# Two query projections of the sparse attention moved between the indexer's dot products

## The reference, cut to what matters

```python
h = rms_norm(x, norm_mix[l])
z = h @ w_in[l]
(g_q, g_k, g_v, g_lr, g_r, d_q, d_k, d_v, i_q, i_k, i_w, c_u) = jnp.split(z, split_at, axis=-1)
dq = rms_norm(d_q.reshape(B, S, DSA_HEADS, DSA_DH), dsa_qnorm[l])    # 6 heads of 64
dk = rms_norm(d_k.reshape(B, S, DSA_HEADS, DSA_DH), dsa_knorm[l])
# per block of 128 queries; qx: 8 indexer heads of 64
dots = jnp.einsum('bthd,bsd->bths', qx, k_idx_f) * (IDX_DIM ** -0.5)
score = jnp.einsum('bths,bth->bts', jax.nn.relu(dots), wx)
score = jnp.where(key_pos[None, :] <= tpos[:, None], score, -jnp.inf)
_, sel = lax.top_k(score, topk)                                      # topk = 128
```

## Time and profile before

| | |
|---|---|
| median of 3 runs | 1573.6 us (1568.34 to 1575.02) |
| span of the profiled execution | 1572.3 us |
| its own whole time | not given beside the span; the span is 1.3 us under the median |
| PE busy | 1479.6 us, 94% |
| DVE busy | 1202.7 us, 76% |
| ACT busy | 884.6 us, 56% |
| POOL busy | 550.9 us, 35% |
| mean granted TensorE clock | 0.971 of full speed |

### The profile page before, as it was taken

The page is one execution under the profiler, slowest core; times in us unless marked ns, Lnnn a source line. Parts: engine busy times, 40 slices in busy tenths (PEclk is TensorE's granted clock), DMA queues, the critical chain, the costliest instruction groups (busy, mean ns, idle before and its releaser), DMA issues.

```text
span 1572.3 us, 20276 instructions
## 1 busy us (share of the span) xinstructions
PE 1479.6 (94%) x6710; PEld 1072.5 (68%) x6710; DVE 1202.7 (76%) x1762; ACT 884.6 (56%) x1286; POOL 550.9 (35%) x250
## 2 busy tenths in 40 slices
PE   7999999999899999999889999989998989999996
PEld 4687565557577888777556865556575778787773
DVE  4697499634469999999758965895335799999997
ACT  5642233563548787888475513235534478878881
POOL 2243113250004665553542421231600046654444
PEclk9999989999889999999999999899999899999998
DMA  6243301230427999999651530013113289999995
GB/s 221 88 107 133 121 1 54 88 103 1 161 100 287 393 398 400 398 399 399 206 181 42 124 129 0 1 54 134 57 35 127 107 322 399 399 399 399 399 399 193
DMA packets 151484, 312.73 MB, mean 199 GB/s; under 512 B 33158, under 2 KB 46380, under 8 KB 151228
## 3 DMA queue, kind: packets, MB, share of 16 engines
q1 hardware_dynamic: 140300, 271.39, 47.6%
q0 software_dynamic: 6624, 24.12, 4.1%
q10 hardware_dynamic: 4496, 16.40, 2.6%
HBM read 287.76 MB, written 29.50 MB: 202 GB/s over the span
## 4 chain that ended last, share of the span: by engine, by line
PE 47%; DVE 26%; DMA 16%; issue 6%; ACT 4%; DVEq 1%; POOL 0%; SPq 0%; POOLq 0%; ACTq 0%
PE ps L654 11%; DMA arena<-in_w_down 11%; DVE rest_w_down L1334 7%; PE ps L671 6%; PE ps L1411 4%; DMA arena<-in_w_gate 3%; DVE rest_w_up L1334 3%; DVE rest_w_gate L1334 3%; PE ps L1433 3%; DVE mixr L1144 2%; PE ps L733 2%; DVE xg_rest L1347 2%; PE ps L674 2%; PE ps L760 2%; ACT head_w_down L1329 2%
## 5 line engine op out<-in xcount | busy, mean ns | idle before, releaser
L1997 POOL TENSOR_TENSOR rest_w_down<-arena,head_w_down 128x2048 fp32r<-128x2048 f32 x30 | 187.6, 6252 | 196.1 <-ACT head_w_down L1329 196.1
L1334 DVE TENSOR_TENSOR rest_w_down<-arena,head_w_down 128x2048 fp32r<-128x2048 f32 x30 | 150.7, 5023 | 14.7 <-ACT head_w_down L1329 14.5
L1334 DVE TENSOR_TENSOR rest_w_gate<-arena,head_w_gate 128x2048 fp32r<-128x2048 f32 x64 | 145.9, 2280 | 0.1
L1334 DVE TENSOR_TENSOR rest_w_up<-arena,head_w_up 128x2048 fp32r<-128x2048 f32 x64 | 143.5, 2282 | 0.1
L1329 ACT ACTIVATE head_w_gate<-arena 128x2048 fp32r<-128x2048 f32 x60 | 115.0, 1920 | 40.7 <-DMA arena<-in_w_gate 40.6
L1329 ACT ACTIVATE head_w_down<-arena 128x2048 fp32r<-128x2048 f32 x60 | 115.2, 1927 | 38.4 <-DMA arena<-in_w_down 37.7
L1329 ACT ACTIVATE head_w_up<-arena 128x2048 fp32r<-128x2048 f32 x64 | 122.1, 1943 | 9.3 <-DMA arena<-in_w_up 9.2
L671 PE MATMUL ps<-hT,arena 128*128 128x512 f32 x224 | 108.6, 616 | 0.0
L1318 PE MATMUL ps<-head_w_gate,xg_head 128*128 128x512 f32 x256 | 104.0, 406 | 4.2 <-DVE xg_rest L1347 3.0
L1308 PE MATMUL ps<-head_w_down,he_head 128*128 128x512 f32 x240 | 99.6, 415 | 6.8 <-DVE rest_w_down L1334 3.7
L1144 DVE SCALAR_TENSOR_TENSOR mixr<-arena,cf,mixr 128x512 f32<-128x512 f32 x120 | 98.4, 820 | 4.3
(11 more groups left out here) (365 smaller groups left out, 3595.9 us busy)
## 6 DMA issues: line engine op xcount, KB each, us to landing
arena<-in_w_gate SPq DMA_DIRECT2D x64, 1024.0 KB, 10.3
arena<-in_w_up SPq DMA_DIRECT2D x64, 1024.0 KB, 11.0
arena<-in_w_down SPq DMA_DIRECT2D x64, 1024.0 KB, 10.5
arena<-in_w_in SPq DMA_DIRECT2D x10, 1536.0 KB, 6.8
yrows<-yb ACTq DMA_DIRECT2D x30, 512.0 KB, 6.3
arena<-in_w_in SPq DMA_DIRECT2D x4, 2048.0 KB, 8.0
x<-in_x SPq DMA_DIRECT2D x8, 512.0 KB, 13.5
arena<-in_w_in SPq DMA_DIRECT2D x16, 256.0 KB, 4.9
```

Of the source, the lines that this page charges most:

```text
L1334: nc.vector.tensor_tensor(wl[q][:, c, :], raw[q][:, c, :], wh[q][:, c, :].bitcast(F32), ALU.subtract).then_inc(s_split[q], 1)
L1997: nc.gpsimd.tensor_tensor(wl[2][:, c, :], raw[2][:, c, :], wh[2][:, c, :].bitcast(F32), ALU.subtract)\
```

## The change

PE's program alone is changed. Job 5 and job 6 are no longer projected behind the dots; behind every second dot stands one chunk of them, three matmuls: 16 chunks behind 16 pairs of dots. `project` and `split_project` take a range of chunks for that. The programs of ACT, DVE, POOL and SP are as before.

```diff
-                def split_project(n):
+                def split_project(n, chunks=range(KD)):
...
-                    for c in range(KD):
+                    for c in chunks:
...
-                    last.then_inc(sN["proj_done"], 1)
+                    if KD - 1 in chunks:
+                        last.then_inc(sN["proj_done"], 1)
...
-                        split_project(n)
+                        split_project(n, chunks)
...
                     nc.tensor.matmul(ps[4 + n % 4][:, 0:P * (i + 1)], iq[r, h // 2, P * i:P * i + P],
                                      ik2[r, 0:P * (i + 1)], start=True, stop=True).then_inc(sN["dots_done"], 1)
+                    if n % 2:
+                        c = n // 2
+                        project(AFTER_IDX + c // KD, range(c % KD, c % KD + 1))
...
-                project(AFTER_IDX)
                 pe.wait_ge(sN["relu_done"], len(DOTS))
                 for n in range(6):
-                    project(AFTER_IDX + 1 + n)
+                    if n:
+                        project(AFTER_IDX + 1 + n)
                     head_sum(n)
```

## The result

The changed kernel takes 1594.6 us (median of 4 runs, 1593.62 to 1601.21), the kernel before beside it 1572.8 (4 runs, 1568.34 to 1575.02). The ratio is 1.0159, 95% interval 1.0133 to 1.0184: slower by 21.7 us, where 11.8 were forecast, and 0.6 us outside the range.

A forecast was written before the change was run, and what follows sets the result against it. PE, busy for 94% of the span, was taken to bound the kernel. ACT's uncovered chain (4.2 us) and the clock (1.7) gave 5.9 us per layer, 11.8 in all, so 1585 us, range 1575 to 1594.

The forecast's parts named there:

- Term 1: PE's dots and projections together: 25.8 us against 26.0 now, row changes of 0.29 us replacing the waits; nothing gained.
- Term 2: ACT's weights head, copy and square no longer hidden behind jobs 5 and 6: first sum of squares 4.2 us late.
- Term 3: PE's clock at half speed for 3.4 us after the new idle stretch of 4.3 us: 1.7 us lost.
- What costs nothing: Part on POOL's rests, DVE's additions (8 us late) and SP's loads, all claimed to add no time.
- PE still sets it: End of the stage at the logits: DVE 1.4 us behind the old start, PE 5.9, so PE sets the end.
- The sign that the prediction named: In the changed timeline, DVE's wait in front of L1122's successor shrinks from 6.65 to about 4.5 us.
- The waits that hold the threes whole: Rival: PE's waits among the dots absorb all three matmuls, dots end as now at 71.4; 1567 us; chance 0.05.
- the free change of rows: Rival: PE's change between half and full rows costs nothing, dots and projections take 21.1 us; 1576 us; chance 0.14.
- the serial pairs: Rival: the two dots of a pair run one after the other, 10.2 us more per layer; 1606 us; chance 0.04.
- the clock stays up: Rival: PE's clock does not fall in the idle stretch, loss 4.2 x 2; 1582 us; chance 0.10.
- The fall of 10.2 us: Rival: PE's clock stays at 0.50 for 10.2 us, loss 9.3 x 2; 1592 us; chance 0.10.

The follow-up runs named there:

- warm_masks: Changed kernel with the selection masks on POOL and 16 idle products on PE before the first sum of squares: 1580.5 us, ratio 1.0053.
- after_masks: Changed kernel with DVE's last step of each top-k, the mask, done by POOL behind its rests: 1588.1 us, ratio 1.0095.
- after_waits: Changed kernel with POOL waiting, before each of its rests, for DVE's mask of the tile before; no work moved: 1587.3 us, ratio 1.0096.
- before_stall: Kernel before with six unread TENSOR_TENSOR instructions of 128x1152 added to POOL where it was idle: 1568.9 us, beside 1571.7.
- fours_masks: Changed kernel with the masks on POOL and six projection matmuls behind every fourth dot instead of three behind every second: 1579.7 us, ratio 1.0049.
- the last order: Changed kernel with one chunk behind every fourth dot, job 6 behind the dots: 1564.7 us with masks on POOL, 1563.3 with POOL's waits.
- act_first_waits: Changed kernel with POOL's waits, and ACT's copy and square of job 5 ahead of the head of dk's weights: 1577.7 us, ratio 1.0032.

## Why the prediction was wrong

**Term 1, the length of dots and projections, held.** 25.8 us forecast, 26.05 measured, both dots of a pair at once, periods of 1.32 to 1.95 us. That nothing is gained by filling the waits is so. The split of the term was less good than its sum: a change between dots and projections cost 0.39 us, not 0.29, and the rest of a pair of 512 keys about 0.88 instead of 0.96.

**Term 2, ACT's chain uncovered, held.** 4.2 us forecast, 30.38 - 25.97 = 4.4 measured, released by ACT's square.

**Term 3, the clock, was too small.** I took 3.4 us of work at 0.50, as at 151.1 in the earlier trace rows; it was 5.3 and 5.5, and `warm_masks` prices it at 2.5 and 2.8 us instead of 1.7.

**The step that failed is in "What costs nothing": "PE still sets it".** The additions ended 8.4 us late, as forecast (8). But I moved DVE's top-k as a block of fixed length. Its 66.2 us from the additions to the end of the normalisations (85.40 - 19.19) became 74.5, because a later DVE meets POOL's rests, which PE's jobs time. The prediction has no term for this collision. Without it DVE ends at 93.8 and the logits come at 99.2; with it at 102.1, and they come at 102.8: 3.6 us, and in layer 1 between 3.7 and 5.0 (103.21 against 99.47 and 98.23). The size in layer 0 is then 4.4 + 2.5 + 3.6 = 10.5 instead of 5.9. These are PE's path and what DVE is behind it. In the changed kernel itself DVE sets the end, and its own path gives the same: 85.4 + 8.4 late + 8.3 held = 102.1. With the longer clock term alone the time would have been 1587 to 1588, as in `after_masks` and `after_waits`, close to the forecast; the collision is the rest.

The trace of the kernel before showed the effect in another place. Timelines of DVE and of POOL in the kernel before:

```profile
42.66 2.80 DVE L1083 SCALAR_TENSOR_TENSOR arena<-arena,scratch 128x512 f32<-128x512 f32 x1 [4.16 <-ACT scratch L941]
...
91.70 0.29 DVE L1107 TENSOR_SCALAR sel<-sel 128x256 f32<-128x256 f32 x1
```

```profile
38.12 6.78 POOL L1247 TENSOR_TENSOR w_rest<-arena,w_head 128x3072 fp32r<-128x3072 f32 x1 [1.90 <-ACT w_head L924]
```

L1083, with two sources in SBUF, took 2.80 us where its like takes 0.69, and ended 0.56 behind POOL's rest. POOL's next rest began at 92.98, 1 us behind the end of the mask at 91.70: the order before kept them apart by little, and a shift of 8.4 us on DVE and 7.0 on POOL, counted from the first dot, undid it. The Trainium skill has the rule, in "GPSIMD Engine Reference", section "8. Key points": POOL shares its SBUF interfaces with VectorE and contends with DVE instructions that take two SBUF inputs or run in a two-port mode. "VectorE: DVE Perf Modes", section "The perf-mode tier table (the rule you actually need)", puts `tensor_scalar` on float32 in SBUF at twice the base rate, and "Why PSUM operands drop a tier" says that an operand in PSUM rules that mode out. The traces agree: the masks are held, while the normalisations, which read PSUM, are not. In `before_stall` they ran from 137.18 beside POOL's sixth instruction, which lasts to 139.11, and took the same 4.66 us for six as in the earlier trace rows. The sign that the prediction named shows the failure: DVE's wait of 6.65 was to shrink to about 4.5; it is 0.50.

**The rivals.** The waits that hold the threes whole, the free change of rows and the serial pairs are refuted by the 26.05 us, by `fours_masks` and by the periods. That the clock stays up is refuted by its 6.8 us at 0.50. The fall of 10.2 us is nearest in the number, 1592, but by luck: the clock was back after 6.8 us, and the missing time is DVE's.

## What to carry to other kernels

Slack of an engine is not a budget that a shift simply uses up: when one engine moves against another, list what its instructions now overlap, DVE's against POOL's first, and look for rows that take longer than their like. An instruction that fills another's waits also uncovers what it covered before; price the serial chain of the engine behind it. If a collision is timed by chance, a wait on the engine that has time can do as much as moving the work: 1587.3 against 1588.1 us here, 1563.3 against 1564.7 in the last order.

## What the runs showed of the hardware

- DVE's TENSOR_SCALAR on float32 in SBUF, when it meets a running POOL TENSOR_TENSOR, ends 0.16 us (256 columns), 0.22 (384) or about 0.25 (512) behind the end of that POOL instruction; one of 0.36 us took 8.79. Between two POOL instructions of 2.18 us it gets in. A rest of POOL that held DVE took 6.80 us, where 6.83 is usual; one that began just behind a mask took 6.98. MAX8 and the SCALAR_TENSOR_TENSOR with a source in PSUM ran on beside POOL (0.70 and 4.66 us for six in `before_stall`).
- Each turn from pairs of float32 dots on 64 rows to rounded matmuls on 128 and back costs PE 0.39 us (26.05 against 22.9 us, 16 turns against 8).
- PE's idle stretches of 1.5 and 2.2 us in `act_first_waits` left the clock at 1.00. Behind 3.6 us in `fours_masks` and 4.2 in the changed kernel it was at 0.50, and so it was behind 2.5 us at 148.4 in the kernel before. In layer 1 of `after_waits` the same 4.2 us cost 1 us less than in layer 0, so the size of the fall varies from one occurrence to the next.
